# POOL's weight splits and row-sum additions of a latent attention in 256-column pieces

## The reference

```
def block(args):
    qn, qp, blk = args
    sc = einsum('bqhd,bkhd->bhqk', qn, k_nope) + einsum('bqhr,bkr->bhqk', qp, kpe)
    sc = where(k_pos[None, :] <= q_pos[:, None], sc * ATT_SCALE, -inf)
    p = softmax(sc, axis=-1)
    return einsum('bhqk,bkhd->bqhd', p, v)
```

## Time and profile before

| | before |
|---|---|
| median of three runs | 3101.9 us (3087.58 to 3104.03) |
| the profiled execution | 3084.0 us, its span 3082.0 us |
| PE busy | 2812.2 us, 91% |
| DVE busy | 1456.9 us, 47% |
| ACT busy | 613.2 us, 20% |
| POOL busy | 1520.5 us, 49% |
| granted clock of TensorE, mean | 0.955 of full speed |

### The profile page before, as it was taken

The page is one execution under the profiler, slowest core; times in us unless marked ns, Lnnn a source line. Parts: engine busy times, 40 slices in busy tenths (PEclk is TensorE's granted clock), DMA queues, the critical chain, the costliest instruction groups (busy, mean ns, idle before and its releaser), DMA issues.

```text
span 3082.0 us, 42736 instructions
## 1 busy us (share of the span) xinstructions
PE 2812.2 (91%) x16960; PEld 2538.5 (82%) x16960; DVE 1456.9 (47%) x2015; ACT 613.2 (20%) x777; POOL 1520.5 (49%) x1593
## 2 busy tenths in 40 slices
PE   5989898989999999999768999998769999999997
PEld 3878887879999999998755666666549999999996
DVE  3441323255444444444765555655335545444444
ACT  4312020341000000001532323222221000000002
POOL 3433323265555555554545646454125566655554
PEclk9999999989999999999888999999879999999998
DMA  5332414132222122221100000002331111111111
GB/s 209 111 98 83 118 61 138 61 89 87 75 87 76 69 75 68 71 81 34 50 32 14 20 12 25 9 23 59 86 100 42 41 48 48 47 47 48 48 41 65
DMA packets 93754, 199.91 MB, mean 65 GB/s; under 512 B 25210, under 2 KB 52218, under 8 KB 92830
## 3 DMA queue, kind: packets, MB, share of 16 engines
q1 hardware_dynamic: 93330, 197.46, 20.1%
q10 hardware_dynamic: 336, 1.25, 0.1%
HBM read 188.07 MB, written 10.61 MB: 64 GB/s over the span
## 4 chain that ended last, share of the span: by engine, by line
PE 86%; DVE 5%; ACT 2%; SPq 2%; POOL 2%; DMA 2%; issue 1%; POOLq 0%; DVEq 0%; ACTq 0%
PE ps L635 69%; PE ps L1803 4%; PE ps L1824 3%; PE ps L594 1%; PE ps L1776 1%; PE ps L1755 1%; DMA w_raw<-in_w_units 1%; PE ps L616 1%; PE ps L1212 1%; PE ps L1721 0%; DMA ada_raw_start<-in_ada_units 0%; PE ps L1203 0%; POOL w_lo L560 0%; PE ps L1222 0%; SPq L2055 0%
## 5 line engine op out<-in xcount | busy, mean ns | idle before, releaser
L555 POOL TENSOR_TENSOR w_hi<-w_raw,ones 128x256 fp32r<-128x256 f32 x684 | 520.5, 793 | 1111.8 <-PE ps L635 880.0
L560 POOL TENSOR_TENSOR w_lo<-w_raw,w_hi 128x256 fp32r<-128x256 f32 x684 | 624.9, 945 | 13.4
L635 PE MATMUL ps<-hn_head_f,w_hi 128*128 128x344 f32 x2112 | 451.5, 322 | 14.7 <-DVE hn_rest_f L800 14.7
L635 PE MATMUL ps<-hn_rest_f,w_hi 128*128 128x344 f32 x2112 | 449.1, 321 | 0.0
L635 PE MATMUL ps<-hn_head_f,w_lo 128*128 128x344 f32 x2112 | 448.0, 321 | 0.0
L635 PEld LDWEIGHTS ps<-hn_head_f,w_hi 128*128 128x128 f32 x2112 | 356.0, 189 | 25.8 <-issue 25.6
L635 PEld LDWEIGHTS ps<-hn_rest_f,w_hi 128*128 128x128 f32 x2112 | 357.5, 189 | 0.0
L635 PEld LDWEIGHTS ps<-hn_head_f,w_lo 128*128 128x128 f32 x2112 | 354.2, 189 | 0.0
L690 DVE SCALAR_TENSOR_TENSOR x<-ps,mod,x 128x688 f32<-128x688 f32 x208 | 194.2, 934 | 336.9 <-PE ps L635 336.9
L635 PE MATMUL ps<-h_head,w_hi 128*128 128x344 f32 x1056 | 224.8, 321 | 7.5 <-DVE h_rest L929 7.5
L635 PE MATMUL ps<-h_head,w_lo 128*128 128x344 f32 x1056 | 225.5, 322 | 0.0
(11 more groups left out here) (415 smaller groups left out, 4460.7 us busy)
## 6 DMA issues: line engine op xcount, KB each, us to landing
w_raw<-in_w_units SPq DMA_DIRECT2D x187, 512.0 KB, 3.5
ada_raw<-in_ada_units SPq DMA_DIRECT2D x96, 512.0 KB, 4.3
ada_raw_start<-in_ada_units SPq DMA_DIRECT2D x16, 512.0 KB, 14.6
x<-in_x SPq DMA_DIRECT2D x8, 516.0 KB, 6.5
row_bcast<-row_scratch SPq DMA_DIRECT2D x4, 1032.0 KB, 6.0
out_y<-y_tiles SPq DMA_DIRECT2D x8, 516.0 KB, 3.0
state_s<-in_state_C SPq DMA_DIRECT2D x4, 1024.0 KB, 8.0
out_C_sample<-state_s SPq DMA_DIRECT2D x4, 1024.0 KB, 12.5
```

The source lines that it names most:

```text
L555: ins = pool.tensor_tensor(hi[s][:, k:k + 2, :], raw[u % 2][:, k:k + 2, :], ones[:, :].unsqueeze(1).to_broadcast([P, 2, P]), ALU.mult)
L560: ins = pool.tensor_tensor(lo[s][:, k:k + 2, :], raw[u % 2][:, k:k + 2, :], hi[s][:, k:k + 2, :].bitcast(F32), ALU.subtract)
L635: mm = nc.tensor.matmul(out(c), w, v[:, a:b], start=(first and p_ == 0), stop=(last and p_ == 2))
```

## The change

`pool_split` and `add` issue the same work in instructions of 256 columns; the semaphore is raised by the last piece alone. `values` units have 256 columns and stay one instruction. What is waited for stays the same.

```
         pool, u, s = nc.gpsimd, U_PAIR + UNIT_AT[name], unit_slot(name)
         h_, l_, r_ = split_rows(name, hi[s]), split_rows(name, lo[s]), unit_rows(name, raw[u % 2])
-        n = 2 if name[0] == "values" else KT
+        n = h_.shape[1]
         pool.wait_ge(w_loaded[u % 2], (u // 2 + 1) * 16)
         if after is not None:
             filled(pool, after)
-        pool.tensor_tensor(h_, r_, ones[:, :].unsqueeze(1).to_broadcast([P, n, P]), ALU.mult).then_inc(w_head, 1)
+        for k in range(0, n, 2):
+            ins = pool.tensor_tensor(h_[:, k:k + 2], r_[:, k:k + 2],
+                                     ones[:, :].unsqueeze(1).to_broadcast([P, 2, P]), ALU.mult)
+        ins.then_inc(w_head, 1)
         pool.wait_ge(w_head, u + 1)
-        pool.tensor_tensor(l_, r_, h_.bitcast(F32), ALU.subtract).then_inc(w_split, 1)
+        for k in range(0, n, 2):
+            ins = pool.tensor_tensor(l_[:, k:k + 2], r_[:, k:k + 2], h_[:, k:k + 2].bitcast(F32), ALU.subtract)
+        ins.then_inc(w_split, 1)
...
                 if j > 1:
                     pool.wait_ge(p_added, later(h, j))
-                pool.tensor_tensor(p0[:, j * P:SEQ], p0[:, j * P:SEQ], probabilities(N, h, j), ALU.add)\
-                    .then_inc(p_added, 1)
+                later_tiles = probabilities(N, h, j)
+                for c in range(j, NCK, 2):
+                    n = min(c + 2, NCK)
+                    ins = pool.tensor_tensor(p0[:, c * P:n * P], p0[:, c * P:n * P],
+                                             later_tiles[:, (c - j) * P:(n - j) * P], ALU.add)
+                ins.then_inc(p_added, 1)
```

## The result

| | before | after |
|---|---|---|
| median, 20 runs each | 3091.05 us (3083.95 to 3104.03) | 3103.45 us (3094.63 to 3113.11) |
| ratio after / before | | 1.003, 95% interval 1.0019 to 1.0041 |
| the profiled execution | 3084.0 us | 3104.64 us, its span 3102.5 us |

The account below looks back on a forecast made before the run. The prediction took TensorE as the bound, 86% of the chain of waits against POOL's 2%. Terms 4.9 + 0.4 + 0.9 + 0.3 = 6.5 us on the median 3101.9 gave 3108.4 us, range 3089 to 3122.

Parts of the forecast that it names:

- second heads of pairs 1 to 6: Attention: POOL's later fifth addition delays the last exponential and TensorE by 0.82 us, six times, 4.9 us.
- pair 0: Second head of the first pair, without `att_rest`: 1.06 us later on POOL against a margin of 0.70, loss 0.36 us.
- last row sums: Last pair's second head: the last row-sum product directly follows POOL's last addition, which ends 0.94 us later.
- first split and the latent: Before the attention: DVE's latent chain takes turns with POOL's pieces, loss 0.3 us; bounds 2.4 gain to 0.3 loss.
- first heads: Even heads of the pairs: taken as nothing, since POOL waits for ScalarE before most additions.
- The mechanism: Second heads: POOL's longer split and additions pass the margin, the last exponential waits for the addition two tiles back, delaying TensorE.
- `att_rest`: DVE subtraction in the attention: about 1.6 us in place of 2.4, without gain as DVE's next instruction waits for TensorE.
- rival "not slower": Semaphore margins hold and DVE gets the port back sooner: 3099.5 us on the median; chance 0.18.
- rival "slower by over 0.5%": POOL becomes the bound of the second heads; reaching 15.5 us needs a piece at 0.21 us; chance 0.10.

Follow-up runs that it names:

- own_last_tile: Changed kernel with each head's last key tile in its own buffer, so its exponential no longer waits for the addition two tiles back; 3095.1 us, ratio 0.9997.
- splits_only: Kernel before with splits in pieces as in the changed kernel, additions whole; 3092.8 us, ratio 0.9994 to before.
- additions_only: Kernel before with additions in pieces as in the changed kernel, splits whole; 3097.1 us, ratio 1.0002 to before.
- additions_128: Changed kernel with additions in pieces of 128 columns, splits still in pieces of 256; 3118.7 us, ratio 1.0078 to before.

## Why the prediction was right

The forecast was a loss of 6.5 us, 0.2%, with terms that could make it 1 to 12; measured are 9.3 us (5.9 to 12.7), 0.3%. The forecast was put on the median of three runs, 3101.9, which lies 8 to 11 us above the later medians of before (3091.05 to 3093.95). So 3108.4 is above the measured 3103.45 by 5 us, though the loss itself was forecast too small: that the base was too high and the loss too low is luck for the absolute number. Step by step:

| step | forecast, us | measured, us |
|---|---|---|
| second heads of pairs 1 to 6 | 4.9 | 6.0 |
| pair 0 | 0.36 | 0.46 |
| last row sums | 0.94 | 1.0 |
| first split and the latent | +0.3 | -0.65 |
| first heads | 0 | 0.2 |
| gaps between heads, TensorE's clock | not in the sum | 3.3 |

Without the gaps 7.0 us are measured against 6.5. Part of that closeness is luck too: the heads and the last row sums came out 1.5 us dearer than forecast, and the first split 0.95 us cheaper.

- **The mechanism** held in each part: POOL's chain of split and additions overruns its margin, ACT's last exponential waits for the addition two tiles back, and TensorE follows. `own_last_tile` shows the wait, `splits_only` and `additions_only` the margin, and `additions_128` that past the margin TensorE follows one for one: by the fifth addition its 11 pieces beyond the changed kernel's at 0.14 us are 1.54 us, and the second head of pair 4 goes from 13.51 to 15.04. That most of the further work is hidden held too: some 31 us of it cost 7.5.
- **The term of the second heads** was mis-sized, 1.00 in place of 0.82. The first addition starts 0.54 us late and not 0.46 (the prediction's own figures, an end at 1916.27 against a start at 1915.76, give 0.51), a piece costs 0.14 and not 0.13 (nine of them 0.1 us), and from the end of POOL's addition to ACT's exponential it takes 0.12 us and not 0.08. About 0.03 us more than forecast are absorbed in POOL's gaps.
- **The first split** has the wrong sign. I priced a turn at 0.53 us for DVE, from the one pair of rows there was the earlier trace rows. In the chain of squares, where each instruction needs the one before, the losses are 0.15, 0.52 and 0.41 three times, and with the two behind them 2.56 us in all against the 3.2 of before; forecast were 3.5. The gain was inside the bounds given.
- **`att_rest`** takes 1.44 us in place of 2.40, and its neighbour then waits 2.69 us for TensorE in place of 1.73. What DVE wins goes nowhere, as the prediction said:

```profile
1926.23 1.44 DVE L2034 TENSOR_TENSOR att_rest<-ada_raw,att_head 128x1024 fp32r<-128x1024 f32 x1
...
1930.36 3.36 DVE L1946 RECIPROCAL row_inv<-ps 128x512 f32<-128x512 f32 x1 [2.69 <-PE ps L1730]
```

- **The rival "not slower"** fell: DVE did get the port back sooner, and it was worth 0.65 us. The Trainium skill (SBUF — State Buffer, Who interferes with whom) says that the ports which the two engines share are an exclusive lock, and that a DVE instruction with two SBUF inputs contends for them with a POOL instruction that reads SBUF. The trace agrees (a square that lasted 3.37 us beside one long instruction lasts 1.75 at most beside pieces), but little of DVE's waiting was on the path.
- **The rival "slower by over 0.5%"** hung on a piece at 0.21 us or more. It costs 0.14. `additions_128` reaches such a loss, 0.8%, with more pieces (21 further ones a head) and not with dearer ones.
- **What was left out** is the clock. The gaps are a third of the loss, and I held TensorE's speed fixed while its waits moved. They could as well have been a gain, as with the additions alone.

## What to carry to other kernels

Cutting an instruction into pieces helps nobody who waits for its result as long as the semaphore stays on the last one; it adds the price of each further piece, here 0.14 us, to whatever chain the instruction stands in. (DVE, which shares the port, did get its turn sooner, but here that was worth 0.65 us.) An engine that is half idle can still set the end, so ask for each wait how much margin it has, and add up everything on that engine between two waits before comparing: an edit that fits into a margin alone, as the splits did, uses it up for the next one. And a prediction to a few microseconds has to allow a few for TensorE's clock as soon as the instants of its waits move.

## What the runs showed that I had not expected

Small shifts in time, of a microsecond or so, moved the stretches of lower clock by whole gaps: 4.77 us at a granted 0.71 where it was 3.60 at 1.00, the same in two separate runs of the changed kernel (4.75 at 0.72), and -2.3 us in another gap when the stalls were placed otherwise. As far as these profiles show, the pattern in the attention belongs to the program and not to the execution: with the splits alone, where the second heads kept their length, every gap is within 0.04 us of before. And a port turn isn't one price: between pieces of 256 columns DVE's instructions lost from 0.15 to 0.52 us.
